# Opening of a two-layer diffusion block: order of modulation chunks, tokens, vectors and first weights

## The chip, the cores and the metric

The kernel runs on one core of one Trainium2 chip. The metric is the device time of one execution in microseconds. The engines of the core are TensorE (PE in the profile), VectorE (DVE), ScalarE (ACT), GpSimd (POOL) and SyncE (SP), which here issues most of the transfers. Each engine works through its own queue in order.

## The reference, cut to what matters

```python
# x (1, 512, 1024), ctx (1, 256, 1024), c (1, 1024), c_ctx (1024,), two layers, float32
silu_c, silu_cc, xc = silu(c), silu(c_ctx), ctx
for l in range(2):
    mod = split((silu_c @ ada_w[l] + ada_b[l])[:, None, :], 6)      # ada_w[l]: 1024 x 6144
    mod_c = split(silu_cc @ ada_w[l] + ada_b[l], 6)
    h = rms_norm(x, mix_pre_g[l]) * (1 + mod[1]) + mod[0]
    hc = rms_norm(xc, mix_pre_g[l]) * (1 + mod_c[1]) + mod_c[0]
    y, yc = even_mixer(h, hc, ...) if l == 0 else odd_mixer(h, hc, ...)   # begins with h @ w_in
    x = x + mod[2] * rms_norm(y, mix_post_g[l])
    h = rms_norm(x, ffn_pre_g[l]) * (1 + mod[4]) + mod[3]
    x = x + mod[5] * rms_norm(conv_ffn(h, ...), ffn_post_g[l])
    # the same for the context xc, while another layer follows
return x
```

The even mixer is a gated convolution over 31 positions beside a two-way mLSTM; the odd one is pooling beside attention. The change touches only what happens before and during the first product of layer 0, `h @ w_in`.

## The kernel before

The 768 tokens (512 latent and 256 context) stay in six tiles `x` of 128 tokens. Large products are made as three passes, high times high, high times low and low times high: ScalarE casts a loaded block of weights `raw` to `w_hi` (`take_high`), VectorE subtracts to get `w_lo` (`take_low`); such a block of 4 x 128 x 256 is a granule, and a unit of 256 output columns takes two. The same split is made of the activations: `h_hi` and `h_lo`, for each of eight blocks k of 128 channels. TensorE runs the units one after the other in `product`; the first four are called conv.

The opening has to bring together four things before `product` can start with k = 0:

- **Tokens.** ScalarE takes the mean square of each tile (`x_squares`), VectorE normalises it (`x_normed`, two buffers `xn`; for a tile j from 2 on it waits until tile j - 2 has been turned), TensorE turns it (`turn_token`), ScalarE copies it to `xT` (`turned_token`).
- **Modulation.** The first 2048 columns of `ada_w[0]` (shift and scale of layer 0) come as eight chunks of 1 MB, 256 columns each. The chunks are numbered o = 0 to 7, an even one for shift and an odd one for scale; pair p = o // 2 serves the blocks k = 2p and 2p + 1. They are loaded in the order `OPENING = (0, 1, 2, 4, 5, 3, 6, 7)` into six buffers, so the seventh and eighth wait for sums 1 and 2. Chunks 0, 1, 4, 5, 6, 7 are multiplied on TensorE with the activated condition (`ada_0_sums(o)`, 16 matmul records of 256 columns), then ScalarE copies two rows (`ada_0_rows`) and TensorE turns them to columns (`ada_0_cols(p)`). Chunks 2 and 3 are summed on VectorE (`ada_1_sums(0)` and `(1)`), and TensorE reduces them with `ada_1_cols`.
- **Vectors.** 19 small transfers (biases, gains, convolution taps) to `vrows`: the first ten from ScalarE's queue, the other nine from SyncE's. TensorE turns them in `turn_vectors`.
- **h.** For each pair p VectorE makes the modulation and `h_32` (`first_mods`), ScalarE `h_hi` (`first_high`), VectorE `h_lo` (`first_low`). `first_ready(k)` is called by `product` before block k.

`kept_busy(n)` issues n matmuls of ones (two records each) whose result nobody reads. The order of all this is written out by hand in each engine's queue. GpSimd clears two marks and then waits for all of h. TensorE's order before the change, in the code:

```python
turn_token(0); turn_token(1); turn_token(2); kept_busy(6); turn_token(3)
ada_0_sums(0); ada_0_sums(1); turn_token(4); turn_vectors(); ada_0_sums(4)
turn_token(5); ada_0_cols(0); ada_0_sums(5); ada_0_sums(6); ada_0_cols(2)
ada_0_sums(7); ada_1_cols()          # then product(conv 0); ada_0_cols(3) before its k = 1
```

Of the kernel before, what the change touches and what calls it, by code (L numbers as in the profile page):

```python
# [34 lines left out]
P = 128  # L35
# [5 lines left out]
NT = T // P  # L41
NL = LAT // P
# [9 lines left out]
N_VECTORS = 19  # L52
# [84 lines left out]


OPENING = (0, 1, 2, 4, 5, 3, 6, 7)

# [57 lines left out]
def build(nc, a, out):  # L200
    U, G, N_GRANULES = plan()
    TOK = token_stages()
    ctx = ExitStack()
    with ctx:
# [22 lines left out]
        x = place("x", [P, NT, D])  # L227
# [114 lines left out]
        x_in = [sem(f"x_in{j}") for j in range(NT)]  # L342
# [121 lines left out]
        def load_vectors(eng, first, end):  # L464

            for q in range(first, end):
                block_, src = vectors[q]
                r = sum(v.shape[0] for b, v in vectors[:q] if b == block_)
                eng.dma_start(vrows[r:r + src.shape[0], block_, :], src).then_inc(sem("vec_in"), 16)

        def load(sp, n, src, i=0):

            sp.wait_ge(low, n + 3 + 4 * i)
            kt = src.shape[1]
            sp.dma_start(raw[:, n % 2, 0:kt, :], src).then_inc(raw_full[n % 2], 16)
# [23 lines left out]
        def _(sp):  # L499
            sp.dma_start(ident[:, :], a["identity"]).then_inc(sem("ident_in"), 16)  # L500

            for s, name in enumerate(("c", "c_ctx")):
                src = a["c"][0] if name == "c" else a["c_ctx"]
                sp.dma_start(vrows[KD * s:KD * (s + 1), 5, :], src.rearrange("(r p) -> r p", p=P)).then_inc(sem("cond_in"), 16)
            for j in range(NT):
                src = a["x"][0, j * P:(j + 1) * P] if j < NL else a["ctx"][0, (j - NL) * P:(j - NL + 1) * P]
                sp.dma_start(x[:, j, :], src).then_inc(x_in[j], 16)

            load_vectors(sp, 10, N_VECTORS)

            def load_ada_0(first, end):

                for pos in range(first, end):
                    o = OPENING[pos]
                    c = o // 2 + 4 * (o % 2)
                    if pos >= 6:
                        sp.wait_ge(ada0_sums, pos - 5)
                    sp.dma_start(ada_0[:, pos % 6], w_ada[0][:, :, c * 256:(c + 1) * 256]).then_inc(ada0_in[o], 16)

            load_ada_0(0, 8)  # L520
            n = G["conv"]
            load(sp, n, w_even[:, 0:4, 512:768])
            load(sp, n + 1, w_even[:, 4:8, 512:768])

            for q in range(4):
                sp.dma_start(gate_b[4 * (q // 2):4 * (q // 2) + 4, 1 - q % 2:2 - q % 2],
# [345 lines left out]
        def _(pe):  # L872
# [6 lines left out]
            def kept_busy(count):  # L879

                for _ in range(count):
                    nc.tensor.matmul(acc[:, U["ada"] % 2, 1, 512:512 + P], ones[:, :], ones[:, :], start=True, stop=True)
# [4 lines left out]
            pe.wait_ge(sem("cond_in"), 32)  # L887
            psum_free(pe, U["cond"])
            transpose(acc[:, U["cond"] % 2, 0, 0:2 * KD], vrows[0:2 * KD, 5, :], 2 * KD).then_inc(unit_done, 1)
            kept_busy(22)  # L890
            u, v = U["xt"], U["ada"]
            psum_free(pe, u)
            psum_free(pe, U["vec"])
# [8 lines left out]
            def turn_token(j):  # L902
                if j >= 2:
                    pe.wait_ge(xt_taken, j - 1)
                pe.wait_ge(xn_ready, j + 1)
                for k in range(KD):
                    last = transpose(acc[:, u % 2, j % 2, k * P:(k + 1) * P], xn[j % 2][:, k * P:(k + 1) * P])
                last.then_inc(xt_full if j < NT - 1 else unit_done, 1)

            def ada_0_sums(o):  # L910

                pe.wait_ge(ada0_in[o], 16)
                c = 512 * (o // 2 % 2) + 256 * (o % 2)
                for k in range(KD):
                    last = nc.tensor.matmul(acc[0:2, v % 2, o // 4, c:c + 256], cond[:, k, :], ada_0[:, OPENING.index(o) % 6, k, :],  # L915
                                            start=(k == 0), stop=(k == KD - 1))
                last.then_inc(ada0_sums, 1)

            def ada_0_cols(p):

                pe.wait_ge(ada0_rows, max(p, 1))
                for c in range(4):
                    at_ = 512 * (p % 2) + 2 * c
                    last = transpose(acc[:, v % 2, p // 2, at_:at_ + 2], ada_r[0:2, c * P:(c + 1) * P], 2)
                last.then_inc(ada0_cols if p < 3 else unit_done, 1)

            def ada_1_cols():

                pe.wait_ge(ada1_sums, 1)
                psum_free(pe, v)  # L930
                for c in range(2):
                    for q in range(2):
                        for x_ in range(2):
                            at_ = 512 + 4 * c + 2 * q + x_
                            last = nc.tensor.matmul(acc[:, v % 2, 0, at_:at_ + 1], ada_p1[:, x_, c, q * P:(q + 1) * P],
                                                    ones[:, 0:1], start=True, stop=True)
                last.then_inc(ada1_cols, 1)

            turn_token(0)
            turn_token(1)  # L940
            turn_token(2)
            kept_busy(6)
            turn_token(3)
            ada_0_sums(0)
            ada_0_sums(1)
            turn_token(4)
            turn_vectors()
            ada_0_sums(4)
            turn_token(5)
            ada_0_cols(0)  # L950
            ada_0_sums(5)
            ada_0_sums(6)
            ada_0_cols(2)
            ada_0_sums(7)
            ada_1_cols()
            h = (h_hi, h_lo)

            def first_ready(k):
                if k == 1:
                    ada_0_cols(3)  # L960
                pe.wait_ge(h0_ready, k + 1)

# [260 lines left out]
        def _(act):  # L1223
# [137 lines left out]
                        x_squares(j, NT + t.chain + j, junk_x[:, :])  # L1361


            load_vectors(act, 0, 10)
            psum_full(act, U["cond"])
            nc.scalar.activation(cond[:, :, :].rearrange("p k s -> p s k"),
                                 acc[:, U["cond"] % 2, 0, 0:2 * KD].rearrange("p (s k) -> p s k", s=2), ACT.Silu
# [28 lines left out]
            def first_high(p):  # L1396

                act.wait_ge(mods0, p + 1)
                for k in (2 * p, 2 * p + 1):
                    for s_, (t0, t1) in enumerate(SEGS[T]):  # L1400
                        last = nc.scalar.activation(h_hi[:, k, t0:t1], xT[:, k, t0:t1], ACT.Identity,
                                                    bias=mods[:, 0, 0, k, s_:s_ + 1], scale=mods[:, 0, 1, k, s_:s_ + 1])
                    last.then_inc(t_high, 1)
# [9 lines left out]
            turned_token(NT - 1)  # L1413
            psum_read(act, U["xt"])
            first_high(0)
            ada_0_rows(2)
            take_high(0)
            ada_0_rows(3)
            take_high(1)
            first_high(1)  # L1420
            first_high(2)
            first_high(3)
            unit_high(2)
# [283 lines left out]
        def _(dve):  # L1707
# [338 lines left out]
            psum_read(dve, U["vec"])  # L2046
            psum_read(dve, U["xt"])
            first_mods(0)
            ada_1_sums(1)
            first_low(0)  # L2050
            take_low(0)
            first_mods(1)
            first_low(1)
            first_mods(2)
# [452 lines left out]
        @block.gpsimd  # L2507
        def _(pool):
            nc.gpsimd.memset(mark[:, 9:10], 0.0).then_inc(low, 4)
            nc.gpsimd.memset(mark[:, 10:11], 0.0).then_inc(ada_used, 4)  # L2510
            pool.wait_ge(h0_ready, KD)
            for first, end in ((0, U_LAT), (U_LAT + LAT, U_CTX), (U_CTX + CTX, U_LEN)):
                ins = nc.gpsimd.memset(conv_u[:, :, first:end], 0.0)
            ins.then_inc(sem("conv_zero"), 1)

            pool.wait_ge(unit_done, U["turned"] + 1)
            pool.wait_ge(sem("m_out"), 32)
            nc.gpsimd.memset(v_tok[:, :, :, HD:VW], 1.0).then_inc(sem("v_ones"), 1)
            for kind, hd, q in ITEMS:
                if kind == "S":  # L2520
                    s_tile = ORDER[q]
                    for e, (d, t0, t1) in STEPS[q]:
                        if t0 <= s_tile * P < t1:

                            pool.wait_ge(sem("e_ready"), 16 * hd + e + 1)
                            block_ = probs[e % 4][:, s_tile * P - t0:s_tile * P - t0 + P]
                            sign = -1 if d else 1
                            nc.gpsimd.affine_select(out=block_, in_=block_, compare_op=ALU.is_ge, fill=0.0, base=0,
                                                    pattern=[[sign, P]], channel_multiplier=-sign).then_inc(sem("e_masked"), 1)

            pool.wait_ge(t_ready, KD + TOK["down02"].chain + NT)
            for v in range(4):
                psum_read(pool, U["in1"] + 1 + v)
                if v >= 2:
                    pool.wait_ge(sem("rot_taken"), v - 1)
                x_ = inb[:, 2 + 2 * v:4 + 2 * v, :] if v < 3 else kT[:, :, 0:LAT]
                for odd in range(2):
                    nc.gpsimd.dma_start(swapped[1 - odd::2, v % 2], x_[odd::2]).then_inc(sem(f"swapped_in{v}"), 16)
# [41 lines left out]
```

## Time and profile before

| what | value |
|---|---|
| median of 3 runs | 1571.29 us (1570.74 to 1572.24) |
| profiled execution | 1571.23 us, span 1569.5 us |
| TensorE busy | 1554.4 us (99%) |
| VectorE busy | 1057.9 us (67%) |
| ScalarE busy | 551.3 us (35%) |
| read from HBM | 166.17 MB |

All times in the rows are microseconds from the start of the span. A timeline row gives start, duration, engine, line, operation, output and inputs, and how many instructions were merged; in brackets stands how long the engine was idle before and what ended the idle time. A busy engine need not set the time: that is read from the chain that ended last.

### The profile page before, as it was taken

Reading aid. Unit: us, or ns where it says so; the run is one execution under the profiler, and the core shown is the slowest. Engines: PE = TensorE matmul, PEld = TensorE weight load, DVE = VectorE, ACT = ScalarE, POOL = GpSimd, SP = SyncE. Lnnn points to the kernel's source line nnn. Section 1 sums busy time; section 2 is a strip of 40 time slices with the busy share of each in tenths; the row PEclk is TensorE's granted clock in tenths of the full one; section 3 lists DMA queues with packets and bytes.
Section 4 is the critical chain, followed back from the end, with each engine's and each line's share of the span. In section 5 each row is a group of like instructions: output and inputs, shape, how many; then the busy total and the mean of one; then the engine's idle time right before and its main releaser. Section 6 shows DMA issues by size and latency. Waiting matters only on the chain.

```text
span 1569.5 us, 21740 instructions
## 1 busy us (share of the span) xinstructions
PE 1554.4 (99%) x8578; PEld 1324.2 (84%) x8578; DVE 1057.9 (67%) x1576; ACT 551.3 (35%) x841; POOL 24.3 (2%) x66
## 2 busy tenths in 40 slices
PE   8999999999999999999999999999999999999998
PEld 5898988778899888888888888988888888888887
DVE  4999999888848883677526437857867543444346
ACT  5423225684722221222211226533326332222233
POOL 0000000220000000000000000000000000000000
PEclk9999999999999999999999999999999999999999
DMA  9622132124135453455233231330022233233232
GB/s 323 207 70 81 55 108 72 63 83 146 41 123 199 160 188 121 148 182 207 93 110 105 62 100 54 125 121 28 1 67 68 87 101 109 79 107 107 81 101 87
DMA packets 132746, 171.54 MB, mean 109 GB/s; under 512 B 16114, under 2 KB 88498, under 8 KB 132666
## 3 DMA queue, kind: packets, MB, share of 16 engines
q1 hardware_dynamic: 131770, 168.25, 33.5%
q0 software_dynamic: 640, 2.10, 0.3%
q8 instruction: 55, 0.90, 0.2%
q14 instruction: 25, 0.20, 0.0%
q10 hardware_dynamic: 256, 0.08, 0.0%
HBM read 166.17 MB, written 2.15 MB: 107 GB/s over the span
## 4 chain that ended last, share of the span: by engine, by line
PE 95%; ACT 2%; DMA 1%; DVE 1%; SPq 0%; issue 0%; POOL 0%; DVEq 0%
PE acc L737 51%; PE acc L786 26%; PE acc L763 5%; PE acc L1213 2%; PE acc L1148 2%; PE acc L1009 2%; PE acc L877 1%; DMA ada<-in_ada_w 1%; PE acc L1161 1%; PE acc L777 1%; PE acc L915 1%; PE acc L1041 1%; ACT probs L1499 1%; PE acc L1118 0%; PE acc L696 0%; PE acc L713 0%
## 5 line engine op out<-in xcount | busy, mean ns | idle before, releaser
L737 PE MATMUL acc<-h_hi,w_hi 128*128 128x512 f32 (+1 forms) x1424 | 494.5, 351 | 0.0
L737 PE MATMUL acc<-h_lo,w_hi 128*128 128x512 f32 (+1 forms) x1424 | 492.5, 350 | 0.0
L737 PE MATMUL acc<-h_hi,w_lo 128*128 128x512 f32 (+1 forms) x1424 | 492.2, 349 | 0.0
L1712 DVE TENSOR_TENSOR w_lo<-raw,w_hi 128x1024 fp32r<-128x1024 f32 x183 | 218.2, 1220 | 135.3 <-ACT w_hi L1233 135.2
L737 PEld LDWEIGHTS acc<-h_hi,w_lo 128*128 128x128 f32 x1424 | 267.1, 189 | 35.1
L737 PEld LDWEIGHTS acc<-h_hi,w_hi 128*128 128x128 f32 x1424 | 267.3, 189 | 34.5
L737 PEld LDWEIGHTS acc<-h_lo,w_hi 128*128 128x128 f32 x1424 | 267.3, 189 | 33.8
L1233 ACT ACTIVATE w_hi<-raw 128x1024 fp32r<-128x1024 f32 x183 | 186.6, 1053 | 214.9 <-PE acc L786 151.7
L786 PE MATMUL acc<-w_hi,hid_hi 128*128 128x512 f32 x434 | 169.5, 391 | 0.0
L786 PE MATMUL acc<-w_hi,hid_lo 128*128 128x512 f32 x434 | 168.9, 389 | 0.0
L786 PE MATMUL acc<-w_lo,hid_hi 128*128 128x512 f32 x434 | 168.8, 389 | 0.0
L1609 ACT ACTIVATE gpad<-acc 128x1024 f32<-128x1024 f32 (+1 forms) x33 | 28.0, 883 | 211.1 <-PE acc L696 95.6
L2341 DVE TENSOR_SCALAR hid<-gpad,ffn_cw 128x512 f32 (+1 forms) x66 | 25.2, 438 | 111.8 <-ACT gpad L1609 111.4
L786 PEld LDWEIGHTS acc<-w_hi,hid_lo 128*128 128x128 f32 x434 | 81.5, 188 | 17.1
L786 PEld LDWEIGHTS acc<-w_lo,hid_hi 128*128 128x128 f32 x434 | 81.5, 188 | 16.7
L786 PEld LDWEIGHTS acc<-w_hi,hid_hi 128*128 128x128 f32 x434 | 81.5, 188 | 16.6
L2085 DVE SCALAR_TENSOR_TENSOR conv_u<-conv_u,dw_w 128x783 f32<-128x783 f32 x90 | 88.3, 1028 | 0.0
L1619 ACT ACTIVATE hid_hi<-hid (+2 forms) x22 | 28.0, 1274 | 146.0 <-DVE hid L1712 146.0
L2339 DVE SCALAR_TENSOR_TENSOR hid<-gpad,ffn_cw,hid 128x512 f32 (+3 forms) x132 | 77.5, 656 | 0.0
L1712 DVE TENSOR_TENSOR hid<-hid,acc 128x1024 f32 (+3 forms) x22 | 32.7, 1487 | 52.4 <-PE acc L737 51.9
L786 PE MATMUL acc<-w_hi,h_hi 128*128 128x512 f32 x160 | 63.5, 397 | 0.0
L786 PE MATMUL acc<-w_hi,h_lo 128*128 128x512 f32 x160 | 62.4, 390 | 0.0
(289 smaller groups left out, 2039.4 us busy)
## 6 DMA issues: line engine op xcount, KB each, us to landing
ada_w<-in_ada_w SPq DMA_DIRECT2D x96, 512.0 KB, 5.5
raw<-in_ffn_w_in SPq DMA_DIRECT2D x88, 512.0 KB, 3.6
raw<-in_ffn_w_out SPq DMA_DIRECT2D x44, 512.0 KB, 4.2
raw<-in_even_w_in SPq DMA_DIRECT2D x24, 512.0 KB, 4.5
ada<-in_ada_w SPq DMA_DIRECT2D x8, 1024.0 KB, 11.9
raw<-in_odd_w_in SPq DMA_DIRECT2D x12, 512.0 KB, 3.5
raw<-in_even_w_out SPq DMA_DIRECT2D x8, 512.0 KB, 5.6
raw<-in_odd_w_out SPq DMA_DIRECT2D x8, 512.0 KB, 4.2
```

What stands on the lines that cost most here:

```text
L737: last = nc.tensor.matmul(acc[:, s, m, t0:t1], w[:, slot, kk, c], x_[:, k, t0:t1], start=(k == 0 and q == 0), stop=(k == KD - 1 and q == 2))
L763: last = nc.tensor.matmul(acc[:, s, m, t0:t1], w_of(m_)[w][:, kk, c], x_[:, k, t0:t1], start=(k == 0 and q == 0), stop=(k == KD - 1 and q ...
L786: last = nc.tensor.matmul(tile_bank(name, a, j), x_[:, k, j * P:(j + 1) * P], w[:, m_ % 4, 2 * kk:2 * kk + 2, :].rearrange("p a c -> p (a ...
L1009: last = nc.tensor.matmul(dst, probs[e % 4][:, t * P - t0:t * P - t0 + P], v_tok[:, ORDER[q], hd, :], start=(q, d, t) == FIRST_TOUCH[b], s ...
L1148: last = nc.tensor.matmul(acc[:, 0, n % 2, t0:t1], inb[:, 2 + hd, i * P:(i + 1) * P], kT[:, hd // 3, t0:t1], start=True, stop=True)
L1213: last = nc.tensor.matmul(acc[:, 1, 1, c:c + P], v1[:, j, (hd // 3) * HD:(hd // 3 + 1) * HD], pT[:, n % 2, j * P:(j + 1) * P], start=(j == ...
L1233: nc.scalar.activation(dst, raw[:, n % 2], ACT.Copy).then_inc(high, 1)
L1609: last = nc.scalar.activation(gpad[:, :, c:c + t1 - t0], acc[:, u % 2, :, t0:t1], ACT.Copy)
L1619: nc.scalar.activation(hid_hi[:, k, 0:tokens], hid[:, k, 0:tokens], ACT.Copy).then_inc(sem("hid_high"), 1)
L1712: return nc.vector.tensor_tensor(out_, in0, in1, op)
L2085: sd.done(nc.vector.scalar_tensor_tensor(dst, src, tap, dst, ALU.mult, ALU.add))
L2339: ins = nc.vector.scalar_tensor_tensor(dst, src, c, dst, ALU.mult, ALU.add)
```

## The change

The changed kernel issues the load of the first modulation chunk (`AHEAD = 1`) ahead of the token tiles, and sums it ahead of the turns. The sum of chunk 1 moves between the turns of tokens 2 and 3. The loads of the first two weight granules move ahead of the seventh and the eighth chunk. The sums of chunks 6 and 7 and `ada_1_cols` move into the first unit, before its k = 2, and `ada_0_cols(3)` from k = 1 to k = 3. ScalarE casts weights earlier in its order, VectorE sums chunk 3 later. The 19 vectors are issued from GpSimd's queue. The dummy matmuls go from 22 to 4 in one place and from 6 to 0 in another.

```diff
--- before.py
+++ after.py
@@ -137,6 +137,7 @@
 
 
 OPENING = (0, 1, 2, 4, 5, 3, 6, 7)
+AHEAD = 1
 
 
 
@@ -502,11 +503,6 @@
             for s, name in enumerate(("c", "c_ctx")):
                 src = a["c"][0] if name == "c" else a["c_ctx"]
                 sp.dma_start(vrows[KD * s:KD * (s + 1), 5, :], src.rearrange("(r p) -> r p", p=P)).then_inc(sem("cond_in"), 16)
-            for j in range(NT):
-                src = a["x"][0, j * P:(j + 1) * P] if j < NL else a["ctx"][0, (j - NL) * P:(j - NL + 1) * P]
-                sp.dma_start(x[:, j, :], src).then_inc(x_in[j], 16)
-
-            load_vectors(sp, 10, N_VECTORS)
 
             def load_ada_0(first, end):
 
@@ -517,10 +513,16 @@
                         sp.wait_ge(ada0_sums, pos - 5)
                     sp.dma_start(ada_0[:, pos % 6], w_ada[0][:, :, c * 256:(c + 1) * 256]).then_inc(ada0_in[o], 16)
 
-            load_ada_0(0, 8)
+            load_ada_0(0, AHEAD)
+            for j in range(NT):
+                src = a["x"][0, j * P:(j + 1) * P] if j < NL else a["ctx"][0, (j - NL) * P:(j - NL + 1) * P]
+                sp.dma_start(x[:, j, :], src).then_inc(x_in[j], 16)
+            load_ada_0(AHEAD, 6)
             n = G["conv"]
             load(sp, n, w_even[:, 0:4, 512:768])
+            load_ada_0(6, 7)
             load(sp, n + 1, w_even[:, 4:8, 512:768])
+            load_ada_0(7, 8)
 
             for q in range(4):
                 sp.dma_start(gate_b[4 * (q // 2):4 * (q // 2) + 4, 1 - q % 2:2 - q % 2],
@@ -887,7 +889,7 @@
             pe.wait_ge(sem("cond_in"), 32)
             psum_free(pe, U["cond"])
             transpose(acc[:, U["cond"] % 2, 0, 0:2 * KD], vrows[0:2 * KD, 5, :], 2 * KD).then_inc(unit_done, 1)
-            kept_busy(22)
+            kept_busy(4)
             u, v = U["xt"], U["ada"]
             psum_free(pe, u)
             psum_free(pe, U["vec"])
@@ -936,27 +938,27 @@
                                                     ones[:, 0:1], start=True, stop=True)
                 last.then_inc(ada1_cols, 1)
 
+            ada_0_sums(0)
             turn_token(0)
             turn_token(1)
             turn_token(2)
-            kept_busy(6)
+            ada_0_sums(1)
             turn_token(3)
-            ada_0_sums(0)
-            ada_0_sums(1)
             turn_token(4)
             turn_vectors()
-            ada_0_sums(4)
             turn_token(5)
             ada_0_cols(0)
+            ada_0_sums(4)
             ada_0_sums(5)
-            ada_0_sums(6)
             ada_0_cols(2)
-            ada_0_sums(7)
-            ada_1_cols()
             h = (h_hi, h_lo)
 
             def first_ready(k):
-                if k == 1:
+                if k == 2:
+                    ada_0_sums(6)
+                    ada_1_cols()
+                    ada_0_sums(7)
+                if k == 3:
                     ada_0_cols(3)
                 pe.wait_ge(h0_ready, k + 1)
 
@@ -1361,7 +1363,6 @@
                         x_squares(j, NT + t.chain + j, junk_x[:, :])
 
 
-            load_vectors(act, 0, 10)
             psum_full(act, U["cond"])
             nc.scalar.activation(cond[:, :, :].rearrange("p k s -> p s k"),
                                  acc[:, U["cond"] % 2, 0, 0:2 * KD].rearrange("p (s k) -> p s k", s=2), ACT.Silu
@@ -1413,11 +1414,11 @@
             turned_token(NT - 1)
             psum_read(act, U["xt"])
             first_high(0)
+            take_high(0)
             ada_0_rows(2)
-            take_high(0)
-            ada_0_rows(3)
             take_high(1)
             first_high(1)
+            ada_0_rows(3)
             first_high(2)
             first_high(3)
             unit_high(2)
@@ -2046,9 +2047,9 @@
             psum_read(dve, U["vec"])
             psum_read(dve, U["xt"])
             first_mods(0)
-            ada_1_sums(1)
             first_low(0)
             take_low(0)
+            ada_1_sums(1)
             first_mods(1)
             first_low(1)
             first_mods(2)
@@ -2508,6 +2509,7 @@
         def _(pool):
             nc.gpsimd.memset(mark[:, 9:10], 0.0).then_inc(low, 4)
             nc.gpsimd.memset(mark[:, 10:11], 0.0).then_inc(ada_used, 4)
+            load_vectors(nc.gpsimd, 0, N_VECTORS)
             pool.wait_ge(h0_ready, KD)
             for first, end in ((0, U_LAT), (U_LAT + LAT, U_CTX), (U_CTX + CTX, U_LEN)):
                 ins = nc.gpsimd.memset(conv_u[:, :, first:end], 0.0)
```

## Rows read from the trace of the kernel before

**Rows 1.** The page's chain that ended last, shares of the span by engine.

```profile
PE 95%; ACT 2%; DMA 1%; DVE 1%; SPq 0%; issue 0%; POOL 0%; DVEq 0%
```

**Rows 2.** Chain in order of time, 0 to 120: start, us, what.

```profile
47.48 31.70 PE acc L737 x180
```

**Rows 3.** Timeline of TensorE, 0 to 75.

```profile
1.14 2.93 PE L882 MATMUL acc<-ones 128*128 128x128 f32 x12 [1.14 <-DVE ones L1982]
...
10.35 1.07 PE L877 MATMUL acc<-ident,xn 128*128 128x128 f32 x8 [0.33 <-DVE xn L1768]
...
14.06 1.50 PE L882 MATMUL acc<-ones 128*128 128x128 f32 x12
...
17.56 7.07 PE L915 MATMUL acc<-ada,cond 128*2 128x256 f32 x32 [1.07 <-DMA ada<-in_ada_w]
...
25.49 0.55 PE L877 MATMUL acc<-ident,vrows 92*128 92x92 f32 x5
26.54 3.62 PE L915 MATMUL acc<-ada,cond 128*2 128x256 f32 x16 [0.49 <-DMA ada<-in_ada_w]
30.09 1.09 PE L877 MATMUL acc<-ident,xn 128*128 128x128 f32 x8
31.11 0.41 PE L877 MATMUL acc<-ident,ada_r 2*128 2x2 f32 x4
...
35.57 3.62 PE L915 MATMUL acc<-ada,cond 128*2 128x256 f32 x16 [0.52 <-DMA ada<-in_ada_w]
...
43.00 1.95 PE L935 MATMUL acc<-ones,ada_p 128*128 128x1 f32 x16
44.81 0.59 PE L737 MATMUL acc<-h_hi,w_hi 128*128 128x512 f32 x2
...
62.35 0.28 PE L737 MATMUL acc<-h_hi,w_hi 128*128 128x256 f32 x1
```

**Rows 4.** Windows: stretch, busy time of each engine (records), granted clock, DMA share, GB/s.

```profile
25.00:30.00 5.00, 4.51 (x28) 2.13 (x25) 4.74 (x12) 1.95 (x7) 0.00 (x0) 1.00 1.10 348
```

**Rows 5.** Timeline of VectorE, 0 to 75, and one row from 75 to 200.

```profile
19.07 0.75 DVE L1768 TENSOR_SCALAR xn<-x,small 128x1024 f32<-128x1024 f32 x1
23.58 0.62 DVE L1996 TENSOR_SCALAR ada_p<-ada,cond 128x256 f32<-128x256 f32 x2 [3.75 <-DMA ada<-in_ada_w]
24.11 5.63 DVE L1999 SCALAR_TENSOR_TENSOR ada_p<-ada,cond,ada_p 128x256 f32<-128x256 f32 x14
32.33 0.17 DVE L1712 TENSOR_TENSOR mods<-acc,vec 128x8 f32<-128x8 f32 x1 [2.59 <-ACT xT L1379]
...
32.73 1.65 DVE L2030 TENSOR_SCALAR h<-xT,mods 128x512 f32<-128x512 f32 x4
...
40.36 1.82 DVE L1712 TENSOR_TENSOR h_lo<-h,h_hi 128x768 fp32r<-128x768 f32 x2
42.09 1.22 DVE L1712 TENSOR_TENSOR w_lo<-raw,w_hi 128x1024 fp32r<-128x1024 f32 x1
...
57.58 2.36 DVE L1712 TENSOR_TENSOR w_lo<-raw,w_hi 128x1024 fp32r<-128x1024 f32 x2
...
118.61 2.36 DVE L1712 TENSOR_TENSOR w_lo<-raw,w_hi 128x1024 fp32r<-128x1024 f32 x2 [1.00 <-ACT w_hi L1233]
```

**Rows 6.** Line 507, token transfers: issue ns min/median/max, first and last start.

```profile
L507 SPq DMA_DIRECT2D x<-in_x x4: 360/432/438, 2.0 to 3.4; - x4
...
DMA to landing us min/median/max: 4.7/7.1/9.5
```

**Rows 7.** Timeline of ScalarE, 0 to 75.

```profile
7.76 1.04 ACT L1256 ACTIVATE junk<-x 128x1024 f32<-128x1024 f32 x1
...
32.78 2.50 ACT L1401 ACTIVATE h_hi<-xT,mods 128x512 fp32r<-128x512 f32 x4 [0.55 <-DVE mods L2024]
...
40.19 1.06 ACT L1233 ACTIVATE w_hi<-raw 128x1024 fp32r<-128x1024 f32 x1 [4.43 <-DMA raw<-in_even_w_in]
```

**Rows 8.** Tile swapped, GpSimd's transfers: issue ns min/median/max, first and last start.

```profile
L2538 POOL DMA_DIRECT2D swapped<-inb x6: 536/536/677, 1008.0 to 1033.8; - x6
```

## Prediction

> **What bounds the kernel now.** I read the chain that ended last first: TensorE holds 95% of it [rows 1], so only what delays TensorE counts. The same chain in order of time shows TensorE without a break from 47.48 us [rows 2]; the change edits only what comes before the end of the first unit. Next I read the timelines of TensorE, VectorE and ScalarE over the first 75 us. The reader should see that until chunk position 1 is in, TensorE waits for transfers; from 35.57 us, when position 6 has landed, it has its own queue of work up to the end of unit 0 at 62.35 us [rows 3]. That 62.35 is the number to follow: all later units follow it on TensorE. I call a chunk by its position in the load order; positions 0 and 1 are chunks 0 and 1, positions 2 and 5 are chunks 2 and 3, summed by VectorE, positions 3, 4, 6, 7 are chunks 4, 5, 6, 7.
>
> **When things land.** Before, position 0 starts TensorE at 17.56, position 3 at 26.54, position 6 at 35.57, each after an idle time that a DMA ended [rows 3]: 9.03 us for three chunks, 3.0 us each, which is 1.05 MB at the 348 GB/s of that stretch [rows 4]. So position 1 lands at about 20.5, position 2 at 23.5 (VectorE starts on it at 23.58 [rows 5]), 4 at 29.5, 5 at 32.5. The first token tile was issued at 2.0 and took the shortest time of the six, 4.7 us [rows 6]: it landed at 6.7. Now position 0 stands ahead of the tokens; it takes the place of two token tiles and lands at about 8.2; the first token lands at 6.7 + 3.0 = 9.7. The same bytes lie ahead of position 1, so it still lands at about 20.5. The first weights come half a chunk (1.5 us) behind position 5, at 34.0; position 6 at 37.0, the second weights at 38.5, position 7 at 41.5.
>
> **The change part by part.** *Fewer dummy matmuls* (36 records fewer in one place, 12 in the other) free TensorE where it would wait anyway: nothing by itself, but their cover goes (clock, below).
>
> *Tokens after position 0.* ScalarE's first squares ran at 7.76 and token 0 was turned at 10.35 [rows 7, 3], 2.6 us later; now 9.7 + 2.6 = 12.3. At the 1.4 us of their landing, tokens 0 to 2 are turned by about 16.4. Then sums(1) stands in the queue and waits for 20.5: 4.1 us idle. Turn 3 is queued behind it, although its token is ready.
>
> *TensorE from 20.5.* A sum of 16 matmuls holds the queue 3.55 us (26.54 to 30.09), a token 1.0 (30.09 to 31.11), the vectors 0.55, a column turn 0.35 [rows 3]. sums(1) to 24.05, turn 3 to 25.05, turn 4 to 26.05, vectors to 26.6, turn 5 to 27.6, columns to 27.95, sums(4) to 31.5, sums(5) to 35.05. All landed in time.
>
> *VectorE from 25.1.* Normalising token 5 waits until token 3 is turned. Before it ran at 19.07, long ahead of need [rows 5]; now reciprocal and scaling (1.0 us) take 25.15 to 26.15. Behind it is queued the first VectorE sum, until now started at 23.58; it takes 6.2 us (0.62 and 5.63 with little overlap [rows 5]), to 32.3. Its cover is gone: the first modulation, which before began at 32.33, begins at the same 32.3, nothing earlier. Then, from rows of before: 0.4 us for mods and 1.65 for h [rows 5]; ScalarE's four h_hi take 2.50 beside it, to 35.2, its weight cast 1.06, to 36.2 [rows 7]; h_lo of two k, 1.82 and some waiting, to 36.3; w_lo 1.22, to 37.5 [rows 5]. The first product starts at 37.5 instead of 44.81. ScalarE's copy for the column turn now stands behind the cast (36.8), the turn is done by 37.2, so it hides.
>
> *Two sums inside unit 0.* The start is 7.3 us earlier, but sums(6), sums(7) and ada_1_cols move into the unit: 3.55 + 3.55 + 1.8 (43.00 to 44.81) = 8.9 us. The unit with its column turn takes 62.35 - 44.81 = 17.55 [rows 3]. 37.5 + 17.55 + 8.9 = 63.95, **1.6 us later than before**. Inside it the waits: sums(6) at 41.8 (landed 37.0), the VectorE sum moved behind w_lo ends at 37.5 + 6.2 = 43.7, needed 45.4; k = 2 restarts at 50.9, h ready 50.3; k = 4 needs its h at 55.5, ready about 55.3 after the second w_lo. Slack 0.2 to 1.7 us each: I cost them at nothing; if the cover goes, at most 1 us.
>
> *After unit 0.* VectorE reaches the next weights at about 60.1 instead of 57.58 [rows 5]. It is nearly without pauses up to 118.61, where it idled 1.00 us for ScalarE [rows 5]. 2.5 - 1.0 = 1.5, no more than TensorE's 1.6; no further loss. SyncE's third weight load is released by w_lo at 37.5, the fourth by w_lo at about 54.4; the next modulation chunks queue behind that, and land from 60 while VectorE wants them at 62.5.
>
> *Vectors on GpSimd's queue.* All 19 loads leave ScalarE and SyncE. The nearest row is GpSimd's own later transfers, 0.54 to 0.68 us each [rows 8]: 19 take 10 to 13 us. With the 9.5 us that the slowest token tile took to land behind a full queue [rows 6] they are in by 23 at the latest, and are needed at 26.05: hidden. What ScalarE saves at the start is hidden too, since it then waits for the tokens. SyncE is released earlier, but its transfers queue behind each other. The bounds are -0.3 us (small packets slow the stream less) and +3 (vectors at 29); I take nothing, by the nearest row.
>
> **The sum.** 63.95 - 62.35 = +1.6 us. The profiled execution took 1571.23 us with a span of 1569.5; the median of the runs is 1571.29, so 1571.29 + 1.6 = 1572.9.
>
> **Rivals.**
> *Full cover.* If VectorE's order cost nothing, TensorE would be busy without a pause from 20.5: 14.9 to the last column turn, then 8.9 + 17.55, so unit 0 ends at 61.85, -0.5 us; with position 1 landing up to 0.8 us earlier, -1.3. For it: enough sums are in TensorE's queue by then. Against it: the order puts token 5's normalisation, and with it VectorE's sum, behind sums(1). 1570.0 to 1570.8. To be faster by over 0.2% (3.1 us) position 1 would have to land before 18, against 348 GB/s.
>
> *The clock, on the slow side.* The granted clock reads 1.00, its 2.4 GHz level, in every stretch, as in [rows 4], yet the first 12 dummy records take 2.93 us and the 12 at 14.06 take 1.50 [rows 3]: at the start the engine works at half pace, the lower level, 1.2 GHz, and reaches full pace near 5.2, having been busy since 1.14. The change idles TensorE from about 5.8 to 8.2 and again from 16.4 to 20.5. Before, the dummies covered such a place and the longest idle was about 1.1 us [rows 3]. If the clock falls in the second gap, sums(1) runs at half pace: 4.1 us until it rises, as at the start, give 2.05 us of work, so +2.05; if all of it stays slow, +3.55. Everything behind shifts: +3.6 to +5.2, 1574.9 to 1576.5. It decides once the loss passes 1.5 us. In the first gap a fall is hidden by the wait for 20.5. Against it: that gap follows 8 us of mostly busy work. The Trainium skill (TensorE: Matmul & The Clock Gate, HAM oscillation) warns that waits for DMA between short bursts put the clock back to half rate; this speaks against the change, and no row here has such a gap.
>
> *Vectors late.* If each took twice the row's 0.6 us they would be issued by 24, land by 28.5 with the shortest time of [rows 6], and the turns behind them would wait 2.4 us: +4, near 1575.3. For it: 19 in a row are in no row, and VectorE's five normalisations of 0.75 us [rows 5] run beside them. The Trainium skill (DMA: Bandwidth & Descriptors, SWDGE vs HWDGE vs iDMA) says that VectorE in its two-port mode locks GpSimd out of the memory it writes such transfers' descriptors to; if all five blocked it, 3.8 us more, the latest case above would end at 26.8, 0.7 us late.
>
> **How the numbers follow.** Forecast (+0.9 to +2.6, 1572.2 to 1573.9) 0.55; full cover 0.17; clock 0.19; vectors late, or a stall inside the unit, 0.06; a gain of over 3.1 us for a reason I don't see 0.03. 0.2%, 3.1 us, is about what this kernel's measurement tells from no change. Faster 0.03, slower 0.24 (the clock, the vectors and a rest), the remaining 0.73 the same. The range reaches from full cover, 1570.0, to near the top of the clock's case, 1576.0.
>
> **What would show it.** Right: the timeline has token 5's normalisation just after the turn of token 3 near 25; the first product at 37 to 38; unit 0's end near 64; the position 1 sum after a pause from 16 to 20.5. Wrong: sums(1) over 4 us long (clock); an idle time before the vectors' turn that GpSimd's transfers ended; the first product before 36; idle time before k = 2, 4 or 6 of the first unit; position 1 landing away from 20.5, which shifts all of it one for one.

## Result and profile after

The changed kernel takes 1573.13 us, median of 20 runs, against 1571.0 for 20 runs of the kernel before: +2.1 us, ratio 1.0017 with a 95% interval of 1.0011 to 1.0023. I had forecast 1572.9. The 20 runs form two groups: 14 at 1572.66 to 1573.57 with a mean granted clock of 0.998 (one 0.999), and 6 at 1575.12 to 1577.04 with 0.994 to 0.996. The profiled execution belongs to the second: 1575.56 us, span 1573.8, against 1571.23 and 1569.5 of before.

TensorE's timeline of the changed kernel, 0 to 75, answering to [rows 3]:

```profile
...
7.43 5.23 PE L917 MATMUL acc<-ada,cond 128*2 128x256 f32 x16 [1.15 <-DMA ada<-in_ada_w]
12.59 1.97 PE L879 MATMUL acc<-ident,xn 128*128 128x128 f32 x16
14.82 1.07 PE L879 MATMUL acc<-ident,xn 128*128 128x128 f32 x8 [0.26 <-ACT xT L1380]
19.12 6.20 PE L917 MATMUL acc<-ada,cond 128*2 128x256 f32 x16 [3.22 <-DMA ada<-in_ada_w]
25.25 1.97 PE L879 MATMUL acc<-ident,xn 128*128 128x128 f32 x16
27.05 0.55 PE L879 MATMUL acc<-ident,vrows 92*128 92x92 f32 x5
27.48 1.07 PE L879 MATMUL acc<-ident,xn 128*128 128x128 f32 x8
28.48 0.41 PE L879 MATMUL acc<-ident,ada_r 2*128 2x2 f32 x4
28.82 7.07 PE L917 MATMUL acc<-ada,cond 128*2 128x256 f32 x32
37.74 0.41 PE L879 MATMUL acc<-ident,ada_r 2*128 2x2 f32 x4 [1.86 <-ACT ada_r L1395]
38.57 0.98 PE L739 MATMUL acc<-h_hi,w_hi 128*128 128x512 f32 x2 [0.42 <-issue]
...
44.27 3.62 PE L917 MATMUL acc<-ada,cond 128*2 128x256 f32 x16
47.81 1.95 PE L937 MATMUL acc<-ones,ada_p 128*128 128x1 f32 x16
49.69 3.61 PE L917 MATMUL acc<-ada,cond 128*2 128x256 f32 x16
53.23 0.62 PE L739 MATMUL acc<-h_hi,w_hi 128*128 128x512 f32 x2
...
66.57 0.28 PE L739 MATMUL acc<-h_hi,w_hi 128*128 128x256 f32 x1
```

Unit 0 ends, with the first record of the next unit, at 66.57 instead of 62.35, 4.22 us later; the whole execution is 4.33 us longer. So all but 0.1 us of it arises before that point. sums(1) starts at 19.12 after 3.22 us of idle time and takes 6.20 us for 16 records, where those at 28.82 take 7.07 for 32. The first product starts at 38.57 after a pause around the column turn of pair 2.

Windows of TensorE over the same stretches, columns: stretch, busy us and records, granted clock, DMA share, GB/s:

```profile
14.00:19.00 5.00, 1.63 (x14) 0.86 1.07 341
19.00:25.00 6.00, 5.88 (x16) 0.55 1.10 348
25.00:38.00 13.00, 11.14 (x71) 1.00 1.10 349
38.00:42.00 4.00, 3.58 (x15) 0.57 0.75 231
42.00:60.00 18.00, 18.00 (x101) 1.00 0.11 32
```

The mean of 0.55 from 19 to 25 and 0.57 from 38 to 42 says that the engine ran at its lower level, 1.2 GHz, for most of both; both follow a wait, of 3.22 us and of 1.86 us. The Trainium skill (TensorE: Matmul & The Clock Gate, HAM oscillation) warns that waits for DMA between short bursts put the clock back to half rate. The trace agrees that a wait comes before each fall, but the work before them was not short: 8.5 us with little idle time (7.43 to 15.89) and 10.6 us (25.25 to 35.89), and the second wait is for ScalarE, not for DMA. The rows also show that the column can miss the lower level at the very start, where nothing has changed yet: sums(0) at 7.43 takes 5.23 us for 16 records, in a window read as 1.00.

VectorE and the transfers, from VectorE's timeline and from GpSimd's:

```profile
18.68 0.75 DVE L1769 TENSOR_SCALAR xn<-x,small 128x1024 f32<-128x1024 f32 x1
26.38 0.16 DVE L1767 RECIPROCAL small<-small 128x1 f32<-128x1 f32 x1 [6.94 <-PE acc L879]
26.58 0.75 DVE L1769 TENSOR_SCALAR xn<-x,small 128x1024 f32<-128x1024 f32 x1
27.25 0.61 DVE L1997 TENSOR_SCALAR ada_p<-ada,cond 128x256 f32<-128x256 f32 x2
...
33.31 0.16 DVE L1713 TENSOR_TENSOR mods<-acc,vec 128x8 f32<-128x8 f32 x1
...
37.24 1.23 DVE L1713 TENSOR_TENSOR w_lo<-raw,w_hi 128x1024 fp32r<-128x1024 f32 x1
...
49.80 0.17 DVE L1713 TENSOR_TENSOR mods<-acc,vec 128x8 f32<-128x8 f32 x1 [5.26 <-PE acc L937]
...
62.40 2.36 DVE L1713 TENSOR_TENSOR w_lo<-raw,w_hi 128x1024 fp32r<-128x1024 f32 x2
```

```profile
1.41 0.68 POOL L470 DMA_DIRECT2D vrows<-in_ada_b  x1 [0.47 <-issue]
2.08 0.54 POOL L470 DMA_DIRECT2D vrows<-in_mix_pre_g  x1
...
11.23 0.53 POOL L470 DMA_DIRECT2D vrows<-in_conv_dw_w  x1
```

Token 5's reciprocal at 26.38 waited 6.94 us for a turn, as forecast, and VectorE's first sum follows at 27.25. From there VectorE has almost no idle time until the first w_lo is done at 38.47, and the product starts at 38.57, although TensorE was through with its sums at 35.89. So the time that sums(1) loses at the lower clock reaches the product through token 5. GpSimd issued its 19 transfers by 11.8 us at 0.49 to 1.06 each; nobody waited for them.

### The profile page after: what moved, and what is told of

Same layout as the page of the kernel before. It is cut to its first block, busy times and chain, and to the rows that moved or that the text cites. A ratio compares the mean times of both kernels' runs of the same rounds, so it can differ in the third digit from the quotient of the medians.

```text
span 1573.8 us, 21644 instructions
## 1 busy us (share of the span) xinstructions
PE 1554.8 (99%) x8530; PEld 1321.2 (84%) x8530; DVE 1057.3 (67%) x1576; ACT 551.1 (35%) x841; POOL 35.0 (2%) x85
## 4 chain that ended last, share of the span: by engine, by line
PE 95%; ACT 2%; DVE 2%; DMA 1%; issue 0%; SPq 0%; POOL 0%; DVEq 0%; ACTq 0%
PE acc L739 51%; PE acc L788 25%; PE acc L765 5%; PE acc L1215 2%; PE acc L1150 2%; PE acc L1011 2%; PE acc L879 2%; PE acc L1163 1%; DMA ada<-in_ada_w 1%; PE acc L917 1%; PE acc L779 1%; PE acc L1043 1%; ACT probs L1500 1%; PE acc L1120 0%; PE acc L698 0%; PE acc L715 0%
```

## Experiments

"Before" is measured again beside each batch: 1571.25, 1571.11 and 1571.15 us. Every kernel was timed 10 or 11 times. The edits are to the changed kernel, where nothing else is said. Theory A was that the clock carries most of the loss, theory B that the order of token 5 behind sums(1) carries it, as the forecast had it.

**Both pauses filled.**

```diff
             turn_token(2)
+            kept_busy(12)
             ada_0_sums(1)
...
             ada_0_sums(5)
+            kept_busy(6)
             ada_0_cols(2)
```

> The changed kernel with 12 dummy matmuls ahead of sums(1) and 6 ahead of the column turn of pair 2, where TensorE idled 3.2 and 1.9 us. Theory A (the clock carries most of the loss): the granted clock stays at 1.000 in every run, sums(1) takes 3.6 us instead of 6.2, the first product starts near 36.2 (now bounded by the landing of the first weights), the median is 1571.2 to 1571.6 and no run lies above 1572.5. Theory B (the order of token 5 behind sums(1) carries it, as forecast): clock 1.000 too, but the median stays at 1572.4 to 1572.9.

Median 1572.42 (1571.53 to 1573.79), +1.2 us, ratio 1.0008 [0.9999, 1.0017]; mean clock 0.998 to 1.000. The low end is theory A's, but 5 of 11 runs lay above 1573.1, so its bound of 1572.5 failed, and so did its clock of 1.000 in every run. The mean clock does not mark the high runs: all five read 0.999, while two runs at 1571.87 and 1572.42 read 0.998. In the profiled execution (1572.02 us) sums(1) took 3.62 us and unit 0 ended at 63.25.

**Only the first pause filled** (the 12 dummies alone).

> Only the 12 dummy matmuls ahead of sums(1). Theory A: the clock may still fall once, in the pause before the first product: some runs at 1571.3 with clock near 1.000, the others up to 1.8 us above, mean clock 0.998 to 0.999. Theory B: 1572.5 as with both gaps filled.

Median 1573.58 (1571.48 to 1574.43), ratio 1.0013 [1.0004, 1.0022]. One run lay near theory A's 1571.3, the other ten at 1573.10 and more, up to 3.1 us above it instead of 1.8. Its windows:

```profile
19.00:25.00 6.00, 5.83 (x38) 1.00 1.11 350
...
38.00:42.00 4.00, 4.00 (x18) 0.69 0.77 241
```

The lower level is gone ahead of and in sums(1) and has stayed in the second place. Unit 0 ended at 64.70, 2.35 later than before. No gain over the changed kernel's lower group: TensorE is done earlier with the sums and then pauses longer, 2.27 us ahead of the column turn instead of 1.86.

**Only the second pause filled** (the 6 dummies alone).

> Only the 6 dummy matmuls ahead of the column turn of pair 2. Theory A: the clock still falls ahead of sums(1); the median stays near 1572.9, mean clock 0.998, but the runs at 1575 and more are gone. Theory B: 1572.9 as well, so this one tells only whether the high runs of the changed kernel come from the second gap.

Median 1573.10 (1571.52 to 1574.22), ratio 1.0011 [1.0002, 1.0020].

```profile
19.00:25.00 6.00, 5.87 (x22) 0.72 1.10 348
...
38.00:42.00 4.00, 4.00 (x24) 1.00 0.80 246
```

As expected: sums(1) still at the lower level (5.30 us), the product at the full one, unit 0 to 64.34; the runs at 1575 and more are gone. Against the version without a fall in its profile (1571.64 us, next) the profiled executions of these two, 1573.41 and 1573.10, are 1.8 and 1.5 us longer: that is about what either fall costs. The profiled execution of the changed kernel, from its upper group, has both, and 3.9 us more. That all six runs of that group had both is likely from their clock of 0.994 to 0.996, but no trace shows it.

**All pauses filled longer:** 10 dummies instead of 4 at the start, 14 and 9 in the two places.

> With 12 and 6 dummies 5 of 11 runs still lay at 1573.2 to 1573.8. Here 10 dummies instead of 4 at the start, 14 ahead of sums(1), 9 ahead of the column turn of pair 2 (there 6 had left 0.73 us idle of the stretch). If the clock is the cause of the high runs, they go: every run below 1572.4, median 1571.6 (what remains against the kernel before, 0.5 us, is the order's). If runs near 1573.5 stay at the same share, something else than idle TensorE makes them.

Median 1571.79, +0.64 us, ratio 1.0006 [0.9997, 1.0015]. Nine of 11 runs at 1571.56 to 1572.05, but two at 1573.36 and 1574.51, whose mean clock reads 1.000 and 0.999. By the expectation the clock is then not what makes all the high runs; what made these two, and the five above with 12 and 6 dummies, isn't shown. The profiled one (1571.64 us) has no window below 1.00 in the opening:

```profile
19.18 3.62 PE L917 MATMUL acc<-ada,cond 128*2 128x256 f32 x16 [0.45 <-DMA ada<-in_ada_w]
...
33.29 2.27 PE L884 MATMUL acc<-ones 128*128 128x128 f32 x18
35.50 0.41 PE L879 MATMUL acc<-ident,ada_r 2*128 2x2 f32 x4
36.12 0.58 PE L739 MATMUL acc<-h_hi,w_hi 128*128 128x512 f32 x2 [0.22 <-issue]
...
45.88 3.62 PE L917 MATMUL acc<-ada,cond 128*2 128x256 f32 x16
...
62.77 0.28 PE L739 MATMUL acc<-h_hi,w_hi 128*128 128x256 f32 x1
```

```profile
23.86 0.16 DVE L1769 RECIPROCAL small<-small 128x1 f32<-128x1 f32 x1 [4.92 <-PE acc L879]
...
24.72 0.61 DVE L1999 TENSOR_SCALAR ada_p<-ada,cond 128x256 f32<-128x256 f32 x2
...
30.79 0.16 DVE L1715 TENSOR_TENSOR mods<-acc,vec 128x8 f32<-128x8 f32 x1
...
34.80 1.23 DVE L1715 TENSOR_TENSOR w_lo<-raw,w_hi 128x1024 fp32r<-128x1024 f32 x1
```

This is what the change costs without the clock: unit 0 ends 0.42 us later than before, and the median is 0.64 us higher, with an interval that still holds 1. Token 5 is late here too (23.86), but VectorE's sum ends at 30.8 because sums(1) started at 19.2.

**Turns 3 and 4 ahead of sums(1).**

```diff
             turn_token(2)
-            ada_0_sums(1)
             turn_token(3)
             turn_token(4)
+            ada_0_sums(1)
```

> The changed kernel with the turns of tokens 3 and 4 ahead of sums(1), no dummies added. Theory A: the turns shorten the idle time ahead of sums(1) (from 3.2 us to pieces under 2 us), so no fall there; VectorE's first sum starts at 23.5 instead of 27.2; the product is bounded by the first weights at 33.9 and starts near 36.2; 1571.2 to 1571.6, unless the clock falls in the then longer pause before the product, which would add up to 1.8 us. Theory B: 1571.3, because it is the order that cost the 1.6 us.

Median 1573.27 (1571.45 to 1575.84), ratio 1.0012 [1.0003, 1.0021]. Theory B's 1571.3 was nearly reached by one run; three of 11 lay under 1572.3. VectorE's sum was early, and then ScalarE's first weight cast had to wait for the landing at 34.2. VectorE, TensorE and ScalarE:

```profile
22.31 0.62 DVE L1997 TENSOR_SCALAR ada_p<-ada,cond 128x256 f32<-128x256 f32 x2 [1.13 <-DMA ada<-in_ada_w]
```

```profile
26.69 7.07 PE L917 MATMUL acc<-ada,cond 128*2 128x256 f32 x32 [1.29 <-DMA ada<-in_ada_w]
```

```profile
34.20 1.06 ACT L1235 ACTIVATE w_hi<-raw 128x1024 fp32r<-128x1024 f32 x1 [2.86 <-DMA raw<-in_even_w_in]
```

TensorE paused 2.03 us ahead of the column turn, and began the product at 36.61, 2.0 us earlier than in the changed kernel, but at the lower level. As the new order opens a new pause, this version does not separate the two theories.

**Vectors back on ScalarE's and SyncE's queues.** `load_vectors(act, 0, 10)` and `load_vectors(sp, 10, N_VECTORS)`, the latter behind the tokens.

> The changed kernel with the 19 vector transfers back on ScalarE's queue (10) and SyncE's (9, behind the tokens). If GpSimd's queue made position 1 land at 19.1 instead of the 20.5 that I had worked out, it lands near 20.5 here, and the time rises by about 1.4 us against the changed kernel (1574.3 median). If the queue is without effect, it lands at 19.1 and the time stays at 1573.

Median 1574.64 (1573.66 to 1578.18), ratio 1.0025 [1.0015, 1.0034]: 1.5 us above the changed kernel. TensorE, then the stream from 12 to 16 us (us, granted clock, DMA share, GB/s), first here and then in the changed kernel:

```profile
20.46 6.40 PE L918 MATMUL acc<-ada,cond 128*2 128x256 f32 x16 [4.74 <-DMA ada<-in_ada_w]
```

```profile
12.00:16.00 4.00, 1.00 1.07 354
```

```profile
12.00:16.00 4.00, 1.00 1.04 363
```

Position 1 lands at 20.46, just where I had worked it out, against 19.12 with GpSimd's queue. The mean rate over 12 to 16 us differs by 9 GB/s only, 0.04 MB, which is 0.1 us, and by no more than 11 GB/s in the other stretches of 4 us from 4 to 20; so most of the 1.3 us is when the last part of position 1 gets through, not how fast bytes flow. The later chunks say the same. With the chunk ahead and GpSimd's queue, position 2 landed at 22.31 (the version with turns 3 and 4 ahead), with the old queues at 23.48 (the chunk ahead alone, below); position 3 landed at 26.69 and 26.38. The lead is gone two chunks later. Why GpSimd's queue changes which bytes come first is open.

**The move into unit 0 without the chunk ahead.** `AHEAD = 0`, the turns, first sums and dummies of the kernel before.

> The changed kernel with AHEAD = 0 and the order of turns and first sums, and the dummies, of the kernel before: what is left is the two sums inside unit 0, the weights ahead of the last chunks and the vectors on GpSimd. Theory B (the chunk ahead with its order costs 1.3 of the 1.6 us): token 5 is normalised near 19, VectorE's sum starts at 23.5, the first product at 36.2 behind the first weights, +0.3 us, 1571.3, clock 1.000. Theory A: the same time, for lack of idle places for the clock to fall. A gain of over 1 us (under 1570) would say that the move into the unit is worth something by itself.

Median 1571.95 (1571.55 to 1573.99), ratio 1.0008 [0.9999, 1.0017]: +0.8 instead of +0.3, no gain. Seven of 11 runs lay at 1571.55 to 1572.14. In the profiled one (1573.91) the clock fell behind the pause of 2.02 us ahead of the column turn. VectorE there:

```profile
23.45 0.62 DVE L1998 TENSOR_SCALAR ada_p<-ada,cond 128x256 f32<-128x256 f32 x2 [4.45 <-DMA ada<-in_ada_w]
...
35.00 1.23 DVE L1714 TENSOR_TENSOR w_lo<-raw,w_hi 128x1024 fp32r<-128x1024 f32 x1 [1.47 <-ACT w_hi L1236]
```

Token 5 was normalised at 18.24 here, long ahead of need, and yet the first w_lo is done at 36.23, no earlier than the 36.03 of the version with all pauses filled. What sets it here is the landing of the first weights, for which ScalarE's cast waited until 33.91. So by these two executions, token 5 behind sums(1) costs about nothing without the clock's fall.

**The chunk ahead alone,** on the kernel before: position 0 loaded ahead of the tokens and summed first, 4 dummies instead of 22.

> The kernel before with position 0 loaded ahead of the tokens and summed first, 4 dummies instead of 22, everything else as it was (6 dummies and turn 3 stay ahead of sums(1)). TensorE is bounded by the landing of position 6 at 35.5 and its own work behind it, as before: +0.0, 1571.0, as long as the clock is up by then. If loading one chunk ahead delays anything that matters, +0.5 to +2.

Median 1571.01 (1570.46 to 1571.31), ratio 0.9998 [0.9989, 1.0007]. As expected, nothing. Here the clock stood at 0.50 from 10 to 12 us, in sums(0) (5.30 us), and it cost nothing, because TensorE waited for position 6 later (idle 0.50 us, start 35.40) as before.

**Vectors on GpSimd alone,** on the kernel before.

> The kernel before with only the 19 vector transfers moved to GpSimd's queue. Positions 0 and 1 land 1 to 1.4 us earlier, but position 6 stays near 35.5 if the stream as a whole is as fast as before, so unit 0 ends at 62.35 and the time stays at 1571.1 plus or minus 0.3. If all positions land earlier by 1 us, TensorE's block of work from position 6 on starts earlier and the time falls by up to 1 us.

Median 1571.38 (1570.90 to 1572.90), ratio 1.0001 [0.9992, 1.0010]: no gain. Windows (us, then busy time and records of TensorE, its weight loads, VectorE, ScalarE and GpSimd, granted clock, DMA share, GB/s):

```profile
24.00:27.00 3.00, 1.34 (x13) 1.15 (x12) 2.71 (x8) 2.17 (x7) 0.00 (x0) 1.00 1.10 348
27.00:31.00 4.00, 3.75 (x10) 1.20 (x11) 3.44 (x9) 0.07 (x1) 0.00 (x0) 0.57 1.10 348
```

In the profiled execution, 1572.90 and the slowest of the 11, position 0 landed 0.7 us earlier than before (16.86), less than expected, and position 3 0.7 us later, at 27.25. TensorE had waited 1.91 us for it, and then ran at 0.57. Unit 0 ended at 64.06, 1.7 us later than before.

**Turns first, first weights earlier.** Turns 3 and 4 ahead of sums(1) and the first granule loaded ahead of position 5.

```diff
-            load_ada_0(AHEAD, 6)
+            load_ada_0(AHEAD, 5)
             n = G["conv"]
             load(sp, n, w_even[:, 0:4, 512:768])
-            load_ada_0(6, 7)
+            load_ada_0(5, 7)
```

> Turns of tokens 3 and 4 ahead of sums(1), and the first weights loaded ahead of the chunk at position 5 as well. The first weights land at 31 instead of 34, the product starts near 34.8, unit 0 ends near 61.3 instead of 62.35: 1569.9 to 1570.3, faster than both kernels by 1 us, unless the clock falls in a pause before the product (then up to 1572).

Median 1570.04, ratio 0.9997 [0.9988, 1.0006]; nine of 11 runs at 1569.33 to 1570.99, two at 1573.70 and 1574.96. The product started at 34.65 and unit 0 ended at 61.40, both as expected. The high runs lie above the 1572 that the clock was allowed for.

**The same, with dummies in its pauses.**

> The version with turns 3 and 4 ahead of sums(1) and the first weights ahead of position 5 (median 1570.04, two of 11 runs at 1573.7 and 1575.0), with dummies in its idle places: 10 at the start, 5 and 4 between the turns, 2 ahead of sums(4), 2 ahead of the column turn. If the clock makes the two high runs, they go: all runs 1569.3 to 1570.4, median 1569.8, 1.3 us under the kernel before. If not, the same spread as without.

Median 1570.33 (1569.82 to 1572.07), ratio 0.9995 [0.9986, 1.0004]. The two high runs are gone, though two of 11 is little to judge by, and the low ones rose by 0.4 us: five runs lie above the expected 1570.4; the profiled one ended unit 0 at 61.08. By medians it is 0.8 us under the kernel before and 2.8 under the changed one; the intervals of both versions hold 1, so a gain over the kernel before is not established.

## Why the prediction came out right, and where it didn't

**The size was right, in part by luck.** I forecast +1.6 us from the order alone and measured +2.1. The runs split it otherwise: without the clock's falls the change costs 0.4 to 0.6 (the filled version), the falls 1.3 to 1.5 more in the median and near 4 in the upper group. The two do not simply add: the fall ahead of sums(1) counts because token 5, and VectorE's work with it, waits behind sums(1). Two errors met and nearly cancelled, which is luck: the step on position 1 was 1.4 us too late, and the clock, a rival at 0.19, came in nearly every run: 19 of 20 read a mean of 0.998 or less, where the kernel before reads 0.999 or 1.000.

**When things land.** "The same bytes lie ahead of position 1, so it still lands at about 20.5" is the step that failed: it landed at 19.12. With the vectors on the old queues it lands at 20.46. My bound for the vectors' term was -0.3 us. The rest of the landing times held: position 0 at 7.43 for 8.2, the first token at 8.67 for 9.7, the first weights by 34.2 for 34.0.

**Token 5 and VectorE's sum.** The order of events held to the letter, the cost did not. I had priced it for a sums(1) at 20.5; at 19.2, without the clock's fall, the first w_lo is done by 36.0 instead of 37.5 (the filled version), and with token 5 on time it is done at 36.2 (the move into unit 0 without the chunk ahead), since the first weights land near 34. So the forecast's path carried only what the clock put on it.

**The unit.** From the first product to its end I had 26.45 us; in the filled version it is 36.12 to 62.77, 26.65. Inside no wait appeared, so the waits that I had costed at nothing did cost nothing.

**After unit 0.** In the changed kernel all is 4.2 to 4.3 us later, and VectorE's idle time at 122.83, [rows 5]'s place, shrank from 1.00 to 0.40 us: no further loss, as said.

**Clock.** The price was about right: sums(1) took 2.6 us more than 3.6 in the changed kernel, within my 2.05 to 3.55, but 1.7 with only the second pause filled and 2.8 with the vectors back. The total that I gave the rival, 1574.9 to 1576.5, fits 5 of the 6 runs of the upper group; the 14 others lie below it. The place was incomplete. I had not counted the pause ahead of the first product, 1.86 us and then 0.42, behind which the clock fell again, though my own numbers held one (sums(5) done at 35.05, ScalarE's copy at 36.8), and I had written that ScalarE's copy for the column turn "hides": its time does, its effect on the clock doesn't. The argument against it, 8 us of mostly busy work before the gap, did not prevent the fall.

**Vectors late** and **full cover** did not happen: the first was excluded by the row of 0.54 us, which held (my "by 23 at the latest" left out the start of the issues near 1.4 us, which changes nothing); the second would have ended unit 0 at 61.85 or, with the early landing, sooner, and even without the clock's falls it ended at 62.77.

**What the change gives up.** No part gains: the chunk ahead alone -0.1 us, the vectors alone +0.2, the move into the unit with them +0.8. Starting the product 6 us earlier is given back in full by the two sums and `ada_1_cols` inside the unit (9.0 us from 44.27 to 53.23), since TensorE has the same work left after position 1.

## What to carry to other kernels

Where one engine has a fixed amount of work behind a landing, an earlier first product is no gain by itself: count what is left for that engine after the last transfer that it waits for. When dummies are removed or a short job is moved out of a wait, look at every pause that this opens, not the longest one, and price the work behind it at the lower clock. In a single execution such a pause may cost nothing, so judge by the spread of many runs. Their mean clock helps, but here some high runs read as full a clock as the low ones. And before pricing a late step, look for the bound that holds without it, here the landing of the first weights.

## What the runs showed of the hardware

The clock fell behind pauses of 1.86 to 4.74 us, but not behind every one: with the vectors back, one execution shows a fall behind its pauses of 4.74 and 1.86 us and none behind 1.87 us ahead of sums(0), which took 3.61 us. Such a fall lengthened sums(1) by 1.7 to 2.8 us and an execution by about 1.5 to 1.8, unless a wait for a transfer behind it takes it up, as with the chunk ahead alone. The granted clock of the profile reads 1.00 before its first change, also where the records run at half pace. And 0.2 MB of small vectors on GpSimd's queue instead of the other two let the second chunk land 1.3 us earlier and the third 1.2, but not the fourth, and the mean rate of the stream is nearly the same.
